# A two-block network kernel: the second mixer rebuilt as a pipeline of 12 score banks, with its units in another order and its output summed per branch

## What is computed

```python
h = x @ w_in[l] + b_in[l]                      # 1024 -> 2328 columns
lru_x, lru_gate, q, kc_raw, vc_raw, ks_, vs_, kw_, vw_, gts = split(h)
# branch 1, a gated linear recurrence over 512 channels
xc  = conv4(lru_x);  r, i = sigmoid(xc @ wa + ba), sigmoid(xc @ wx + bx)
log_a = -8 * r * softplus(-lam);  a = exp(log_a)
u = sqrt(-expm1(2 * log_a)) * (i * xc)
y_lru = scan(a, u) * gelu(gate)
# branch 2, attention with 8 heads of 64, two key groups, three kinds
kc, vc = compress(kc_raw), compress(vc_raw)    # 15 blocks of 32 tokens, a small MLP
y_nsa = g0 * attend(q, kc, vc) + g1 * attend(q, ks_, vs_) + g2 * attend(q, kw_, vw_)
mix = concat([rms_norm(y_lru, gn_lru), rms_norm(y_nsa, gn_nsa)]) @ w_out[l]
x = layer_norm(alpha * x + mix)
```

## Time and profile before

| | us |
|---|---|
| median of 3 runs | 3297.05 |
| lowest, highest | 3292.52, 3299.48 |
| the profiled execution, its time | 3293.3 |
| its span | 3291.5 |
| mean granted TensorE clock, share of full | 0.92 |
| PE busy | 2933.0 |
| DVE busy | 2234.2 |
| ACT busy | 1606.3 |

### The profile page before, as it was taken

How to read it: one execution, slowest core, us unless ns; L and a number is a source line. 1 busy time by engine, 2 the same in 40 slices (tenths; PEclk the granted TensorE clock), 3 DMA queues, 4 the chain that set the end, 5 groups by cost and what they waited for, 6 DMA issues and landing times.

```text
span 3291.5 us, 47819 instructions
## 1 busy us (share of the span) xinstructions
PE 2933.0 (89%) x18672; PEld 2659.1 (81%) x18672; DVE 2234.2 (68%) x3820; ACT 1606.3 (49%) x2646; POOL 60.8 (2%) x115
## 2 busy tenths in 40 slices
PE   5787799898898966999998999988589999989998
PEld 4676698776797856989998888878489999978886
DVE  4765676675554354689775788853549897758887
ACT  4435444334443343456776445533334667744553
POOL 1000000010000000000000000000000000000000
PEclk8898899899899767999999999987599999999999
DMA  7323576584466302556656777761045665667775
GB/s 246 96 78 109 172 253 231 179 274 129 141 185 198 117 20 93 178 183 203 188 182 201 236 241 242 240 204 39 13 155 177 197 198 183 185 218 242 243 241 166
DMA packets 213697, 582.34 MB, mean 177 GB/s; under 512 B 24321, under 2 KB 89889, under 8 KB 212193
## 3 DMA queue, kind: packets, MB, share of 16 engines
q1 hardware_dynamic: 163856, 496.25, 48.2%
q0 software_dynamic: 12752, 49.47, 4.5%
q10 hardware_dynamic: 36864, 33.57, 3.0%
HBM read 542.49 MB, written 36.70 MB: 176 GB/s over the span
## 4 chain that ended last, share of the span: by engine, by line
PE 78%; DVE 14%; ACT 4%; DMA 2%; issue 2%; ACTq 0%; POOL 0%; DVEq 0%; SPq 0%; POOLq 0%
PE psum L569 76%; DVE gmem L1759 3%; DVE wr L1759 3%; ACT gmem L1241 2%; DVE gmem L1762 2%; DVE gmem L2492 1%; ACT L1241 1%; ACT wr L1241 1%; PE psum L612 1%; DVE xmem L1762 1%; DVE gmem L2489 1%; DMA raw<-in_ada_w 1%; DMA xmem<-gs 0%; DVE gmem L1755 0%; DVE gmem L2494 0%
## 5 line engine op out<-in xcount | busy, mean ns | idle before, releaser
L1759 DVE TENSOR_TENSOR wr<-raw,wr 128x1024 fp32r<-128x1024 f32 (+1 forms) x878 | 1070.1, 1221 | 688.2 <-ACT wr L1241 687.6
L569 PE MATMUL psum<-xr,wr 128*128 128x256 f32 x10464 | 1335.8, 289 | 27.6 <-DVE wr L1759 12.2
L569 PEld LDWEIGHTS psum<-xr,wr 128*128 128x128 f32 x10464 | 1302.5, 197 | 39.1 <-issue 15.7
L1241 ACT ACTIVATE wr<-raw 128x1024 fp32r<-128x1024 f32 (+1 forms) x878 | 918.9, 1048 | 355.1 <-PE psum L569 326.7
L569 PE MATMUL psum<-wr,cr 128*128 128x512 f32 x3360 | 785.2, 395 | 52.5 <-DVE wr L1759 28.1
L569 PEld LDWEIGHTS psum<-wr,cr 128*128 128x128 f32 x3360 | 638.4, 191 | 190.5 <-ACT cr L1241 24.5
L569 PE MATMUL psum<-gmem 128*128 128x128 f32 (+7 forms) x1640 | 249.7, 308 | 56.1 <-DVE gmem L1759 35.9
L1241 ACT ACTIVATE cr<-xmem 128x256 fp32r<-128x256 f32 x256 | 107.2, 419 | 368.8 <-PE psum L569 345.7
L569 PEld LDWEIGHTS psum<-gmem 128*128 128x128 f32 (+2 forms) x1640 | 217.7, 212 | 85.7 <-DVE gmem L1759 33.7
L569 PE MATMUL psum<-wr,xr 128*128 128x512 f32 (+1 forms) x960 | 235.2, 403 | 18.7 <-DVE xr L1759 13.9
L569 PEld LDWEIGHTS psum<-wr,xr 128*128 128x128 f32 x960 | 182.0, 197 | 64.4 <-DVE xr L1759 14.9
(11 more groups left out here) (131 smaller groups left out, 1464.5 us busy)
## 6 DMA issues: line engine op xcount, KB each, us to landing
raw<-in_uv SPq DMA_DIRECT2D x512, 512.0 KB, 4.7
raw<-in_ffn_in SPq DMA_DIRECT2D x88, 512.0 KB, 4.3
gs<-xmem ACTq DMA_DIRECT2D x256, 128.0 KB, 3.3
xmem<-gs SPq DMA_DIRECT2D x256, 128.0 KB, 4.4
raw<-in_ada_w SPq DMA_DIRECT2D x48, 512.0 KB, 3.7
gmem<-in_ada_w POOLq DMA_DIRECT2D x48, 512.0 KB, 4.9
raw<-in_ffn_out SPq DMA_DIRECT2D x44, 512.0 KB, 3.7
raw<-in_ret_a SPq DMA_DIRECT2D x32, 512.0 KB, 4.4
```

Source lines behind the costliest of these rows:

```text
L569: ins = pe.matmul(o, a, b, start=first and i == 0, stop=final and i == len(pairs) - 1, skip_group_check=skip)
L1241: return act.activation(o, a, func, **k)
L1759: return dve.tensor_tensor(o, a, b, op)
```

## The change

- **Order of units.** The columns of `w_in` come as compress inputs first (12, 15), then the recurrence's inputs (0 to 3), keys (13, 14), then the row units, then queries (8 to 11), and the recurrence's gate (4 to 7) last, inside the attention.
- **Attention by banks.** The 32 pairs of branch, query half and head make 12 banks of scores (`BANKS`), 512 columns each: two heads where a=1, four where a=0. For each bank PE first writes the penalty with one matmul of an identity by the table (`al_r`, rounded by POOL beforehand), then adds the scores. DVE takes the maximum of that bank alone from PSUM, ACT the exponentials from PSUM to `ering`, PE transposes, DVE or ACT copies by turns, PE multiplies by the values. Scores of bank st+3 are issued at bank st; a gate unit goes in at st = 0 to 3.
- **Compression.** Its inputs (`kin`) are made by POOL with eight small adds, laid out so that one product over 128 rows replaces two over 64.
- **Recurrence.** Its steps stand one by one in the order, beside units. The root is sqrt((1+a²)t), with a² as a square on ACT; the reciprocal is gone. softplus of lambda is taken once for both layers in the prologue.
- **Output per branch.** The gains of the norms go into the weights, in the split of their units (`scaled`). The rms scale of a row is applied to the sums after the product. The recurrence's half (4 units, `mix_out_a`, in two column halves) goes in at st = 6, 7, 9 and 10; its root is a Newton iteration on DVE. `my` starts as alpha*x, made by POOL. The attention's half is four `mix_out` units at the end.

```diff
+MIX_COLS = (12, 15, 0, 1, 2, 3, 13, 14, 8, 9, 10, 11, 4, 5, 6, 7)
...
+        for n in range(2):
+            for i in range(2):
+                scaled[len(units)] = [(512 * k, 512 * k + 512, col(f"gnl{l}", 2 * i + k)) for k in range(2)]
+                units.append((dr["w_out2a"][l, n, i], UNIT))
+        for k in range(4, 8):
+            scaled[len(units)] = [(0, UNIT, col(f"gnn{l}", k - 4))]
+            units.append((w_out2[k], UNIT))
...
+    def mixer2(s, l):
+        s["mix_start"](l)
+        for i in range(8):
+            s["mix_col"](l, i)
+            if i >= 4:
+                s["mix_conv"](l, i - 4)
+            if i == 5:
+                s["cmp_hidden"](l)
+            if i == 6:
+                s["cmp_out"](l)
+        s["mix_rows"](l, 0)
+        s["lru_gates"](l)
+        s["mix_rows"](l, 1)
+        s["mix_rows"](l, 2)
+        s["lru_decay"](l)
+        s["mix_col"](l, 8)
+        s["lru_powers"](l)
+        s["mix_col"](l, 9)
+        s["lru_input"](l)
+        s["mix_col"](l, 10)
+        s["mix_col"](l, 11)
+        s["cmp_scores"](l)
+        for st in range(3):
+            s["att_scores"](l, st)
+            s["att_exp"](l, st)
+        s["lru_scan"](l)
+        for st in range(12):
+            s["att_turn"](l, st)
+            if st + 3 < 12:
+                s["att_scores"](l, st + 3)
+            if st < 4:
+                s["mix_col"](l, 12 + st)
+            if st == 9:
+                s["mix_sum_a"](l, 0)
+            if st in (6, 7, 9, 10):
+                s["mix_out_a"](l, st // 9, (st - 6) % 3)
+            if st == 0:
+                s["cmp_turn"](l)
+            if st == 1:
+                s["cmp_values"](l)
+            if st > 0:
+                s["att_values"](l, st - 1)
+            if st + 3 < 12:
+                s["att_exp"](l, st + 3)
+            if st == 4:
+                s["lru_y"](l)
+            if st == 7:
+                s["lru_norm"](l)
+            if st == 9:
+                s["nsa_turn"](l, 1)
+        s["att_values"](l, 11)
+        s["mix_sum_a"](l, 1)
+        s["nsa_turn"](l, 0)
+        for k in range(4, 8):
+            s["mix_out"](l, k)
...
+        def att_scores(l, st):
+            br, a, h0, nh, w_, _ = bank_of(st)
+            b = 2 + st % 3
+            claim(b)
+            pe.wait_ge(*zeroed[l, "alibi"])
+            mm(bank(b), [(ident_r, al[a][:, h0:h0 + nh, :])], True, False, True)
+            o = bank(b).rearrange("p (h s) -> p h s", h=nh)
+            for i in range(nh):
+                pr, m = head(h0 + i)
+                ins = mm(o[:, i, :], [(nqT[pr, m, quarter(a)], kv[pr, 1 + br, 0:w_])], False, i == nh - 1, True)
+            ins.then_inc(*S.pe.up(("z", l, st)))
+            drained[b] = S.act["e", l, st]
...
+        def att_exp(l, st):
+            br, a, h0, nh, w_, _ = bank_of(st)
+            dve.wait_ge(*S.pe["z", l, st])
+            dve.tensor_reduce(nmx[:, br, a, h0:h0 + nh], bank(2 + st % 3).rearrange("p (h s) -> p h s", h=nh), AX.X,
+                              ALU.max, negate=True).then_inc(*S.dve.up(("max", l, st)))
...
+        def lru_input(l):
+
+            dve.wait_ge(*L.act["a2", l])
+            stt(ra, a2, 1.0, ra, ALU.add, ALU.mult).then_inc(*L.dve.up(("u2", l)))
...
-            dve.reciprocal(xc, xc).then_inc(*L.dve.up())
...
+        def mix_sum_a(l, n):
+            dve.wait_ge(*L.dve["rms", l])
+            dve.wait_ge(*done())
+            dve.wait_ge(*zeroed[l, "my"])
+            for a in range(2):
+                v = my[:, a, 512 * n:512 * n + 512]
+                stt(v, bank(a), rn[:, a:a + 1], v, ALU.mult, ALU.add).then_inc(*X.dve.up(("out a", l, n, a)))
...
+                        pool.tensor_tensor(kin[r, i, 16 * half:16 * half + 16, 15 * g:15 * g + 15],
+                                           k4[:, :, half:half + 15], pb,
+                                           ALU.add).then_inc(*kin_made.up(l if i + g + half == 3 else None))
...
+            pool.tensor_copy(alr[:, 0:3072], alib).then_inc(*zeroed.up((l, "alibi")))
+            pool.tensor_scalar(my, x, ALPHA, None, ALU.mult).then_inc(*zeroed.up((l, "my")))
```

More of the change, by code:

```diff
@@ L253, in const @@
         return dr["cst"][:, o:o + (n or k)]
-    units = []
+    units, scaled = [], {}
     for part in (0, 1):
@@ new lines, in mix_out_a, with lru_norm @@
+        def mix_out_a(l, n, i):
+            if i == 0:
+                claim(0, 1)
+            pe.wait_ge(*L.dve["lo", l])
+            row_unit((0, 1), xr, i, 2, 512, 2, 2)
+            for a in range(2):
+                drained[a] = X.dve["out a", l, n, a]
+        def lru_norm(l):
+            claim(2)
+            pe.wait_ge(*L.act["sq", l])
+            for a in range(2):
+                ins = mm(bank(2)[:, a:a + 1], [(ra[:, m, quarter(a)], ones[:, 0:1]) for m in range(4)])
+            ins.then_inc(*L.pe.up(("ss", l)))
+            drained[2] = L.dve["ss", l]
@@ L1638, in mix_turn, with lru_norm, cmp_scores, cmp_turn @@
-        def mix_turn(l):
-            for k0 in range(0, 8, 4):
-                act.wait_ge(*S.dve["mix", l])
-                act.wait_ge(*L.dve["mix", l])
-                f(xr[:, 0, k0:k0 + 4, :], mix[:, k0:k0 + 4, :], AF.Copy).then_inc(*N.act.up(("mix", l, k0)))
+        def lru_norm(l):
+            pass
+        def cmp_scores(l):
+            act.wait_ge(*S.dve["d", l])
+            e = csc[:, :, :, 0:15]
+            f(e, e, AF.Exp).then_inc(*S.act.up(("ce", l)))
+        def cmp_turn(l):
+            act.wait_ge(*S.pe["pt", l])
+            f(pcT.rearrange("p j t -> p (j t)"), bank(6), AF.Copy).then_inc(*S.act.up(("pt", l)))
@@ new lines, in att_turn, with att_values, mix_out_a, mix_sum_a @@
+        def att_turn(l, st):
+            if st % 2:
+                act.wait_ge(*S.pe["t", l, st])
+                if st >= 4:
+                    act.wait_ge(*S.pe["o", l, st - 4])
+                f(tring[st % 4], bank(5 + st % 2), AF.Copy).then_inc(*S.act.up(("t", l, st)))
+        def att_values(l, st):
+            pass
+        def mix_out_a(l, n, i):
+            split()
+        def mix_sum_a(l, n):
+            pass
+        def nsa_turn(l, a):
+            act.wait_ge(*S.dve["sum", l, a])
+            if a == 0:
+                act.wait_ge(*S.act["ss", l, 1])
+            f(nscr, onsa[:, a, :], AF.Square, accum_out=rn[:, 2 + a:3 + a]).then_inc(*S.act.up(("ss", l, a)))
+            hi_of(("on", l), xr, a, 1, 4 - a)
+            if a == 0:
+                root(S, ("on", l), rn[:, 2:4])
@@ L1831, in prologue @@
             split()
+            for l in range(2):
+                ts(lam8[:, 4 * l:4 * l + 4], col(f"lam{l}", 0, 4), -1.0, None, ALU.mult).then_inc(*L.dve.up())
+                ts(qb8[:, 4 * l:4 * l + 4], col(f"bin{l}", 8, 4), 0.125, None, ALU.mult).then_inc(*L.dve.up())
+            softplus(L, "lam", lam8, lamt)
+            own(L)
+            ts(lam8, lam8, -8.0, None, ALU.mult).then_inc(*L.dve.up("lam"))
         def modulate(m, q):
@@ new lines, in mix_conv @@
+        def mix_conv(l, m):
+            d = xc[:, m, :]
+            dve.wait_ge(*X.act["col", l, 2 + m])
+            dve.wait_ge(*zeroed[l, "pad"])
+            for j in range(4):
+                s, wc = lcb[:, m, j:j + 256], col(f"conv{l}", j * 4 + m)
+                if j == 0:
+                    ts(d, s, wc, col(f"convb{l}", m), ALU.mult, ALU.add).then_inc(*L.dve.up())
+                else:
+                    own(L)
+                    stt(d, s, wc, d, ALU.mult, ALU.add).then_inc(*L.dve.up(("xc", l) if m == j == 3 else None))
@@ new lines, in cmp_hidden, with cmp_out @@
+        def cmp_hidden(l):
+            pass
+        def cmp_out(l):
+            dve.wait_ge(cmp_in[l], 64)
+            dve.wait_ge(*S.pe["kv", l])
+            dve.wait_ge(*S.act["kc", l])
+            tt(vct, bank(6)[:, 128:256], b2v, ALU.add).then_inc(*S.dve.up(("vc", l)))
+            own(S)
+            tt(vcb, bc(vct.rearrange("p (g e) -> p g e", g=2).unsqueeze(2), [P, 2, 4, 64]),
+               bc(rmask.unsqueeze(1).unsqueeze(3), [P, 2, 4, 64]), ALU.mult).then_inc(*S.dve.up(("vcb", l)))
@@ new lines, in cmp_weights @@
+        def cmp_weights(l):
+            e = csc[:, :, :, 0:15]
+            mx, sm_, inv = (cmx[:, i] for i in range(3))
+            dve.wait_ge(*S.act["ce", l])
+            dve.tensor_reduce(sm_, e, AX.X, ALU.add).then_inc(*S.dve.up())
+            own(S)
+            dve.reciprocal(inv, sm_).then_inc(*S.dve.up())
+            dve.wait_ge(*S.act["gates", l])
+            own(S)
+            tt(inv, inv, gate3[:, :, :, 0], ALU.mult).then_inc(*S.dve.up())
+            own(S)
+            tt(inv, inv, bc(cmpv.unsqueeze(2), [P, 2, 8]), ALU.mult).then_inc(*S.dve.up())
+            own(S)
+            tt(e, e, bc(inv.unsqueeze(3), [P, 2, 8, 15]), ALU.mult).then_inc(*S.dve.up(("p", l)))
```

877 lines of the change are left out of this document (365 added, 512 removed).

## The result

The changed kernel took 3185.3 us (median of 4 runs, 3184.21 to 3188.92) beside 3296.89 us of before: a ratio of 0.9665, 95% interval [0.9648, 0.9681], so 111.6 us or 3.4% less. The forecast was 3180 us, with a range from 3132 to 3238.

The account below looks back on a forecast made before the run. PE's work on weights was taken to bound the kernel, with savings only in the two mixers, which lose time to PE idling and a low clock. 3293.3 - 116 + 1 = 3178.3 us profiled, given as 3180, range 3132 to 3238.

Parts of the forecast that it names:

- The mixer's length: Each of the second network's two mixers: 166 us summed over seven stages plus 4 for clock dips, 170 us.
- The third, fourth and sixth stage: Compressed scores to first softmax, 12 us; banks 0 to 3 with gate units, 27; banks 9 to 11, 13.
- the first stage: Units 0 to 7, compression, rows and gates: 47.6 us, plus 4.4 for a slow unit and the gelu, 52 us.
- a faster POOL gains nothing; I take 0: POOL's adds, penalty table and alpha*x all have slack, so their speed was costed at 0 us.
- Compression's POOL adds hidden: Eight adds on POOL start at 7 us, are wanted at 18.6, so are hidden up to 1.4 us each.
- The wait for banks 0 and 1: Banks 9 to 11: PE waits 3 us while DVE empties them after the Newton root, copy and maximum queued behind.
- DVE isn't busy enough for this to count beyond the stages above: Work removed on DVE, the 6.5 us reciprocal, full-width maxima and gains, was given no further saving.
- Prologue: Softplus before the third split: small operations and two table loads, paced by DMA arrivals, 0 to 6 us, taken as 1.
- Nothing waits: Rival: stages two to six run at PE's own work, 147 us a mixer, 3134 us; 8%.
- Lock step: Rival: each bank's steps run one behind the other, 5.35 us a bank, 200 us a mixer, 3240 us; 5%.
- POOL was in time: Against the rival that the compression waits for POOL's adds, slower than before beyond 8.6 us an add; 2%.
- the slow-clock rival: Clock stays low from bank 0 on: the 61 us become some 107, a mixer 212 us, 3262 us; 6%.

Follow-up runs that it names:

- my_act: The changed kernel with alpha*x made by ACT behind the units of the gates in place of POOL: 3169.46 us, 0.9625 of the kernel before.
- both_moved: The changed kernel with alpha*x on ACT and the compression's eight adds on DVE, both in place of POOL: 3173.02 us, 0.9622 of before.
- sum_8: The changed kernel with alpha*x on ACT, row sums of squares one bank earlier, and the first two output units' drain at bank 8, not 9: 3163.63 us.
- recip_back: The changed kernel with the recurrence's root as before, with the reciprocal on DVE and no square on ACT: 3200.84 us, 0.9718 of before.
- ahead_1: The changed kernel with scores issued one bank ahead in place of three, units staying where they are: 3238.11 us, 0.9825 of before.
- kin_dve: The changed kernel with the compression's eight adds on DVE in place of POOL, alpha*x staying on POOL: 3172.6 us, 0.9625 of before.
- norm_early: The changed kernel with alpha*x on ACT and the recurrence's row sums of squares one bank earlier: 3169.62 us, 0.9619 of before.

## Why the prediction held, step by step

**The mixer's length.** 170 us forecast, 172.2 and 169.6 measured. By stages of l = 0, forecast and then measured: 52 and 52.2; 19 and 17.3; 12 and 13.7; 27 and 29.0; 24 and 24.1; 13 and 16.3; 19 and 19.6. The third, fourth and sixth stage ran over by 7.0 us together, at a clock of 0.57, 0.85 and 0.79, and the second was 1.7 us short; the 4 us for clock dips cover most of that. How much of the 7.0 is the clock, and how much the small matmuls that I priced too low (below), no run separates.

**But the first stage is right by luck: its errors cancel.** I took 12 us for the compression products and they took 7.7: the 128 took 221 ns each in the mean, and "the second of a pair slow" didn't hold. The 4.4 us for a slow unit behind the compression and for the gelu didn't come either: that unit took 3.13 us, and PE waited for nothing there. These 8.7 us came back in a wait that my sum didn't have, 5.9 us at the gate products, and in the 6.46 us that these then took (3.4 forecast). The step that failed is "a faster POOL gains nothing; I take 0". I had costed POOL's adds and looked for slack of its results; I hadn't asked what POOL's work does to DVE's. There the contention stood in the prediction as "perhaps 5 us more per mixer"; my_act shows 6 to 7, with the slow gate products. The prediction had splits and convolutions stretched a little; what cost most was one operation that stood still until POOL was done.

**Compression's POOL adds hidden**: right. They took 1.12 us each (8.98 for eight) and were done 1.5 us before the first compression product, which waited for none of them, and both_moved is no faster than my_act. They lengthen a split of DVE to 1.7 us now and then, which PE doesn't feel.

**Sizes inside the stages.** Penalty matmuls took 7.0 us, not 3: one alone, between others, takes 0.47 us at the full clock and 0.79 at the half, not the 0.25 of a row of twelve. The scores of 256 columns alone took 12.8 us, where I had 10 for all. The four stages from the compressed scores to bank 11 came to 83.1 us, where I had 76 and 4 for dips, and these two terms are in them.

**The wait for banks 0 and 1**: forecast 3 us for the Newton root with copy and maximum behind it; measured 2.62, and 1.5 us more because the unit behind it ran at a lower clock. But the reason was half wrong: the drain, not the root, stood too far back (sum_8).

**The reciprocal**: "DVE isn't busy enough for this to count beyond the stages above". It is in the stages, and recip_back prices the old root at 7.8 us a mixer, in front of the compressed scores.

**Prologue**: 1 us taken, 0 measured (interval from -3 to +3 us). **Scaled splits**: no cost is seen; they weren't tried alone.

**The rivals.** "Nothing waits", 3134 us, is 25 us below what the best kernel here reached, whose mixers lasted 155.9 and 157.8 us: the chain at the end (1.6 us of waits before the output's last part, twice, and a turn) and ACT's second stage remain. Lock step was forecast at 3240 us; ahead_1, with one bank ahead, has 3238. That the two agree is partly chance: the rival took 5.35 us for a bank and 3 us for each unit on top, where ahead_1 has 8.7 us for a bank without a unit and 5.5 for the next, and 11.5 us of the first mixer's 26.8 are slower matmuls, which the rival didn't price. The clock stayed high, and POOL was in time.

**Two slips in the working.** The three stages from bank 0 to bank 11 are 27, 24 and 13, which is 64 us and not 61; the forecast was added up from the stages, so only the price of the slow-clock rival hangs on it. And the 6.27 us in the chain are sixteen exponentials and their sixteen reads (x32 in the earlier trace rows), as the lock-step rival says, and not eight.

**What was to be seen**: table loads 8 in a mixer; PE's wait for ACT before the compressed scores 1.02 us; PE idle 20.4 us in the first mixer and 19.9 in the second. The clock over 0.85 from bank 0 to the output held only in part: 0.85, 0.93 and 0.79.

## What to carry to other kernels

When work is given to an idle engine, ask not only whether its result is in time, but which instructions of the other engines run beside it, and whether PE waits for one of them soon after: the same collision cost 6 to 7 us a mixer here, and nothing when it came 7 to 10 us earlier. A pipeline of small steps needs as much work ahead as the round trip through the other engines takes, and no more: one bank ahead lost nearly half the gain, two were as good as three by the times, and with three ahead it didn't matter whether units stood between. A wait of PE is to be priced with what follows it, since the matmuls behind it may run at the lower clock: in ahead_1's first mixer 15.3 us more of idle time came with 11.5 us of slower matmuls.

## What the hardware showed

POOL and DVE hold each other up. POOL's multiplication of 128x2048 f32 by a constant kept DVE's operation of 0.41 us for 5.46, and POOL's cast of 128x3072 kept a split of 1.03 us for 3.21 (both above). DVE's operation finished 0.14 and 0.15 us behind POOL's recorded end, in the two mixers, and 0.15 us behind it in the second mixer of kin_dve; it wasn't merely slowed. The other way round, POOL's cast of 128x128 takes 0.29 us in the changed kernel and took 1.26 in the first mixer of kin_dve, beside a split of DVE. The Trainium skill describes this on the page "SBUF — State Buffer", section "SBUF: two separate sides": for a DVE instruction in a two-port mode or with two SBUF inputs, the port pair that both engines share is "an exclusive lock, not a bandwidth split", held for the whole instruction of the one that starts first. The trace agrees in these three places. In the first mixer of kin_dve it agrees only in part: the first of DVE's three operations was held for 3.80 us and was done 1.45 us ahead of POOL's recorded end (1089.38 us), and the other two ran in what was left, the last of them done 0.4 us ahead of it:

```profile
1084.13 3.80 DVE L1836 SCALAR_TENSOR_TENSOR gmem<-gmem,cols 128x256 f32<-128x256 f32 x1
```

Spans on POOL are rough, and whether that is all of it stays open.

POOL took 1.12 us for an add of 64x240 f32 that took DVE 4.36/8 = 0.55 us (kin_dve): a factor of two, as the Trainium skill's page "GPSIMD Engine Reference", section "8. Key points", says of elementwise work.

The granted clock doesn't follow from the wait before a matmul alone. In sum_8 the first output unit stood behind a wait of 1.24 us in both mixers; it took 2.99 us in the first, at 1.00, and 4.58 in the second, at 0.61, though PE had been busy at 1.00 for all of the 13 us ahead of the wait in both. What decides it stays open. So differences of 2 to 3 us within one mixer can't be put down to one wait; norm_early's first mixer lasted 2.5 us longer than my_act's and its second 3.4 us less.
